# Differential-attention scores as pairs of half-array matmuls, both softmaxes side by side

## The reference, cut to what matters

```python
scale = DIFF_HEAD_DIM ** -0.5            # DIFF_HEAD_DIM = 64
for start in range(0, S, Q_BLOCK):       # Q_BLOCK = 128
    s = jnp.einsum('bqhrd,bkhrd->bhrqk', qb, kb).astype(jnp.float32) * scale   # r = 0, 1
    mask = jnp.arange(end)[None, :] <= (start + jnp.arange(Q_BLOCK))[:, None]
    p = jax.nn.softmax(jnp.where(mask, s, -jnp.inf), axis=-1)
    attn = p[:, :, 0] - lam * p[:, :, 1]
    outs.append(jnp.einsum('bhqk,bkhe->bqhe', attn.astype(vb.dtype), vb))
```

## Time and profile before

| | |
|---|---|
| median of three runs | 3796.17 us |
| lowest, highest | 3788.92, 3796.29 us |
| the profiled execution's own time | 3797.9 us |
| its span (first to last instruction) | 3795.5 us |
| mean granted TensorE clock | 0.993 |
| bytes moved by DMA | 799.34 MB |

### The profile page before, as it was taken

The page is one execution under the profiler, slowest core; times in us unless marked ns, Lnnn a source line. Parts: engine busy times, 40 slices in busy tenths (PEclk is TensorE's granted clock), DMA queues, the critical chain, the costliest instruction groups (busy, mean ns, idle before and its releaser), DMA issues.

```text
span 3795.5 us, 58631 instructions
## 1 busy us (share of the span) xinstructions
PE 3710.7 (98%) x24136; PEld 3092.0 (81%) x24136; DVE 1834.5 (48%) x3358; ACT 1378.4 (36%) x2500; POOL 482.8 (13%) x244
## 2 busy tenths in 40 slices
PE   8989999999999999998999999999999999999999
PEld 7878878978897887976888779888777888887887
DVE  5757534541645355557655665555654222232223
ACT  4322422231232354566656555545552200021001
POOL 2101220000000000233233430100000100000000
PEclk9999999999999999999999999999999999999999
DMA  8746677467665877866676666554424655464554
GB/s 313 266 161 228 228 269 268 178 222 239 217 216 183 281 248 233 283 213 203 223 232 233 199 212 214 173 160 162 140 110 169 238 188 187 176 240 172 190 195 160
DMA packets 198874, 799.34 MB, mean 211 GB/s; under 512 B 20816, under 2 KB 70224, under 8 KB 130384
## 3 DMA queue, kind: packets, MB, share of 16 engines
q1 hardware_dynamic: 198608, 795.59, 60.3%
HBM read 594.18 MB, written 201.33 MB: 210 GB/s over the span
## 4 chain that ended last, share of the span: by engine, by line
PE 90%; DVE 4%; ACT 2%; DMA 1%; issue 1%; SPq 0%; POOL 0%; DVEq 0%; ACTq 0%
PE bank L1402 86%; PE bank L1406 4%; DVE P L2484 1%; DVE P L2486 1%; DVE R L2145 0%; SPq L2688 0%; ACT P L1940 0%; ACT P L1939 0%; ACT slot L1823 0%; POOL slot L2648 0%; DMA zraw<-in_x_t_dram 0%; DMA R<-X1d 0%; DMA slot<-Wd 0%; DVE Z1a L2192 0%; ACT L1939 0%
## 5 line engine op out<-in xcount | busy, mean ns | idle before, releaser
L1402 PE MATMUL bank<-Z1a,slot 128*128 128x512 f32 x3048 | 781.6, 401 | 9.5 <-DVE slot L2083 9.5
L1402 PE MATMUL bank<-Z1b,slot 128*128 128x512 f32 x3048 | 785.2, 402 | 4.0 <-DVE Z1b L2192 3.8
L1402 PE MATMUL bank<-slot,Z0b 128*128 128x512 f32 (+1 forms) x3504 | 708.7, 353 | 8.1 <-DVE AF L2214 5.3
L1402 PEld LDWEIGHTS bank<-Z1b,slot 128*128 128x128 f32 x3048 | 567.3, 189 | 139.7 <-issue 7.5
L1402 PEld LDWEIGHTS bank<-Z1a,slot 128*128 128x128 f32 x3048 | 566.0, 189 | 140.0 <-DVE slot L2083 9.5
L1402 PEld LDWEIGHTS bank<-slot,Z0b 128*128 128x128 f32 x3504 | 562.8, 189 | 101.1 <-DVE AF L2214 6.0
L2648 POOL TENSOR_TENSOR slot<-raw,slot 128x1024 fp32r<-128x1024 f32 x117 | 308.2, 2642 | 676.7 <-ACT slot L1823 676.6
L2145 DVE SCALAR_TENSOR_TENSOR R<-bank,small,R 128x512 f32<-128x512 f32 x352 | 260.9, 749 | 208.4 <-PE bank L1402 207.8
L1402 PE MATMUL bank<-KS,DQ 128*128 128x512 f32 (+3 forms) x960 | 281.8, 389 | 9.9 <-DMA KS<-Kd 5.5
L2452 DVE TENSOR_SCALAR_CACHE_REDUCE P<-bank 128x512 f32<-128x512 f32 (+3 forms) x320 | 189.3, 608 | 201.3 <-PE bank L1402 201.0
L2660 POOL TENSOR_TENSOR Z0b<-AF,Z0b 128x512 fp32r<-128x512 f32 x88 | 127.5, 1449 | 1235.9 <-ACT Z0b L2013 1235.9
(11 more groups left out here) (235 smaller groups left out, 4560.8 us busy)
## 6 DMA issues: line engine op xcount, KB each, us to landing
slot<-Wd SPq DMA_DIRECT2D x390, 1024.0 KB, 4.9
Wd<-slot SPq DMA_DIRECT2D x130, 1024.0 KB, 7.4
raw<-in_wts_dram SPq DMA_DIRECT2D x130, 512.0 KB, 4.2
DQ<-Qd SPq DMA_DIRECT2D x192, 128.0 KB, 3.7
DV<-Vd SPq DMA_DIRECT2D x60, 256.0 KB, 4.6
KS<-Kd SPq DMA_DIRECT2D x24, 512.0 KB, 7.3
KS<-Kd SPq DMA_DIRECT2D x24, 384.0 KB, 7.0
zraw<-Yd SPq DMA_DIRECT2D x16, 512.0 KB, 5.0
```

The costliest lines, as they stand in the source:

```text
L1402: return e.matmul(o, a, b, start=start, stop=stop, skip_group_check=True)
```

## The change

For diff heads, `scores` for r = 0 only waits, and for r = 1 a new function `score_pair` computes chunk c of both softmaxes. KS is laid out the other way round: softmax 0's keys lie in partitions 0 to 63, softmax 1's in 64 to 127, the high parts in one buffer and the low parts in another. DQ holds softmax 0's query parts in partitions 0 to 63 and softmax 1's in 64 to 127, in two slots. Each matmul contracts 64 rows, softmax 0 in the upper half of the array and softmax 1 in the lower, into two banks. Three products are taken (high x high, low x high, high x low; low x low is left out), two matmuls each. In the last chunk both masks come first. VectorE waits for softmax 1's signal for both. The planner's `front` has c outside and r inside, new modelled costs, one slack of 2000 ns in place of 300, and asks for the next head's second K part after the unit's last chunk of both softmaxes. Stick-breaking heads keep their matmuls. NKS is a name for the three buffers.

```diff
@@ -41,6 +41,7 @@
 N_TILES = 64 + N_F
 NSLOT, NRAW = 4, 2
 C_CUT = 14
+NKS = 3
 
 
 class Signal:
@@ -199,7 +200,7 @@
             for qt in range(NT)]
 
 
-SLACK_H, SLACK_C, SLACK_F, SLACK_B = 1500.0, 2000.0, 300.0, 2500.0
+SLACK_H, SLACK_C, SLACK_F, SLACK_B = 1500.0, 2000.0, 2000.0, 2500.0
 
 
 class Order:
@@ -646,6 +647,7 @@
         self.banks.remove(6)
         yield ("ev", self.user[6])
         P.put(("att",), ("pool", 200), ("dve", 600))
+        held = [0.0, 0.0]
         for u, (s, e, half, qt) in enumerate(self.units):
             i = self.heads.index((s, e))
             if (half, qt) == (0, 0):
@@ -658,32 +660,31 @@
                 yield ("tr", u - 2, (NT * self.units[u - 2][0] + self.units[u - 2][3]) // 4)
             n = SUB * s + 128 * (qt + 1)
             ws = chunks(n)
-            for r in ((0, 1) if e < 4 else (half,)):
-                yield max(P.end[("ld", i, "k", r)], P.end[("ld", i, "q", qt)])
-                for c, w in enumerate(ws):
-                    m = len(self.chunk_no)
-                    self.chunk_no[u, r, c] = m
-                    if m > 1:
-                        yield t2
-                    if m:
-                        t2 = t1
+            yield max([P.end[("ld", i, "k", r)] for r in ((0, 1) if e < 4 else (half,))] + [P.end[("ld", i, "q", qt)]])
+            for c, w in enumerate(ws):
+                for r in (0, 1) if e < 4 else (half,):
+                    self.chunk_no[u, r, c] = len(self.chunk_no)
+                    if e >= 4 or r == 0:
+                        yield held[0 if e < 4 else -2]
+                    if e >= 4:
+                        pe = 30 + 0.92 * w + (60 if c == len(ws) - 1 else 0)
                     else:
-                        t2 = 0.0
-                    ev = ("dve", 90 + 1.2 * w) if e < 4 else ("act", 400 + 1.7 * w)
-                    t1 = P.put(("sc", u, r, c), ("pe", 30 + 0.92 * w + (60 if c == len(ws) - 1 else 0)), ev,
-                               after=P.clock["pe"])
-                if qt == NT - 1 and r == 0:
-                    self.get(i + 1, ("k", 1))
-                if r == 1:
-                    self.get(i + 1, ("q", qt))
-                if e < 4:
-                    t = P.put(("ex", u, r), ("dve", 120), ("act", 500 + 0.9 * n), after=t1)
+                        pe = 80 + 1.37 * w + (120 if c == len(ws) - 1 else 0) if r else 0
+                    t = P.put(("sc", u, r, c), ("pe", pe), ("dve", 90 + 1.2 * w) if e < 4 else ("act", 400 + 1.7 * w),
+                              after=P.clock["pe"])
+                    held = [held[1], t]
+            if qt == NT - 1:
+                self.get(i + 1, ("k", 1))
+            if e < 4 or half:
+                self.get(i + 1, ("q", qt))
             if e < 4:
+                for r in range(2):
+                    t = P.put(("ex", u, r), ("dve", 120), ("act", 500 + 0.9 * n), after=t)
                 yield t
                 P.put(("cb", u), ("dve", 900 + 1.1 * n), after=t)
             else:
-                yield t1
-                P.put(("cb", u), ("dve", 300 + 3.5 * n), after=t1)
+                yield t
+                P.put(("cb", u), ("dve", 300 + 3.5 * n), after=t)
 
     def back(self):
         P = self.P
...
@@ -1336,7 +1337,7 @@
 
             s, e = HEADS[i]
             u = UNITS.index((s, e, 0 if e < 4 else r, qt))
-            return pe_sc("sc", u, r, len(chunks(SUB * s + 128 * (qt + 1))) - 1)
+            return pe_sc("sc", u, r if e >= 4 else 1, len(chunks(SUB * s + 128 * (qt + 1))) - 1)
 
         def last_values(i, g):
             s, e = HEADS[i]
@@ -1591,18 +1592,42 @@
                 n = SUB * s + 128 * (qt + 1)
                 ws = chunks(n)
                 w, at = ws[c], sum(ws[:c])
-                ks = KS[plan.kloads.index((i, r)) % 3]
-                b = bank[2 + plan.chunk_no[u, r, c] % 2]
                 if u == 0:
                     first_layer_done(pe)
                 if (free := score_free(u, r, c)) is not None:
                     pe.wait_ge(*free)
-                pe.wait_ge(*d_ks[plan.kloads.index((i, r)) % 3]("ld", i, "k", r))
                 pe.wait_ge(*d_dq[qt]("ld", i, "q", qt))
+                if e_ < 4:
+                    if r == 1:
+                        score_pair(u, c)
+                    return
+                ks = KS[plan.kloads.index((i, r)) % NKS]
+                b = bank[2 + plan.chunk_no[u, r, c] % 2]
+                pe.wait_ge(*d_ks[plan.kloads.index((i, r)) % NKS]("ld", i, "k", r))
                 mm(b[:, 0:w], DQ[:, qt, 2 * r, :], ks[:, at:at + w], True, False)
                 if c == len(ws) - 1:
-                    mm(b[:, w - 128:w], ident_bf[:, :], mask_bf[:, 0 if e_ < 4 else 1, :], False, False)
+                    mm(b[:, w - 128:w], ident_bf[:, :], mask_bf[:, 1, :], False, False)
                 mm(b[:, 0:w], DQ[:, qt, 2 * r + 1, :], ks[:, at:at + w], False, True).then_inc(*pe_sc.inc("sc", u, r, c))
+
+            def score_pair(u, c):
+
+                s, e_, half, qt = UNITS[u]
+                i = HEADS.index((s, e_))
+                ws = chunks(SUB * s + 128 * (qt + 1))
+                w, at = ws[c], sum(ws[:c])
+                m = [plan.kloads.index((i, part)) % NKS for part in range(2)]
+                b = [bank[2 + plan.chunk_no[u, r, c] % 2][:, 0:w] for r in range(2)]
+                last = c == len(ws) - 1
+                if last:
+                    for r in range(2):
+                        mm(b[r][:, w - 128:w], ident_bf[:, :], mask_bf[:, 0, :], True, False)
+                for n, (q, k) in enumerate(((0, 0), (1, 0), (0, 1))):
+                    pe.wait_ge(*d_ks[m[k]]("ld", i, "k", k))
+                    for r in range(2):
+                        h = slice(64 * r, 64 * r + 64)
+                        x = mm(b[r], DQ[h, qt, q, :], KS[m[k]][h, at:at + w], n == 0 and not last, n == 2)
+                        if n == 2:
+                            x.then_inc(*pe_sc.inc("sc", u, r, c))
 
             def transposes(u, g):
                 st = ("tr", u, g)
@@ -2444,7 +2469,7 @@
                     return
                 ws = chunks(SUB * s + 128 * (qt + 1))
                 at, w = sum(ws[:c]), ws[c]
-                dve.wait_ge(*pe_sc("sc", u, r, c))
+                dve.wait_ge(*pe_sc("sc", u, 1, c))
                 if r == 0:
                     probabilities_free(dve, u)
                 elif u:
@@ -2790,17 +2815,17 @@
                 s, e_ = HEADS[i]
                 if what == "k":
                     m = plan.kloads.index((i, x))
-                    if m >= 3:
-                        sp.wait_ge(*last_score(*plan.kloads[m - 3], NT - 1))
+                    if m >= NKS:
+                        sp.wait_ge(*last_score(*plan.kloads[m - NKS], NT - 1))
                     else:
                         first_layer_done(sp)
                     for z in range(s + 1):
                         stored(z, 2 + 2 * e_ if e_ < 4 else 6 + 2 * e_, 0)
                     n = SUB * (s + 1)
-                    d = d_ks[m % 3]
-                    for part in range(2):
-                        to = KS[m % 3][64 * part:64 * part + 64, 0:n].bitcast(F32)
-                        transfer(to, Kd[e_, 64 * x:64 * x + 64, part, 0:n], d, "ld", i, what, x)
+                    for y in range(2):
+                        h, src = (x, y) if e_ >= 4 else (y, x)
+                        to = KS[m % NKS][64 * y:64 * y + 64, 0:n].bitcast(F32)
+                        transfer(to, Kd[e_, 64 * h:64 * h + 64, src, 0:n], d_ks[m % NKS], "ld", i, what, x)
                 elif what == "q":
                     if i:
                         sp.wait_ge(*last_score(i - 1, 1, x))
@@ -2808,6 +2833,10 @@
                         first_layer_done(sp)
                     stored(s, 3 + 2 * e_ if e_ < 4 else 7 + 2 * e_, 0)
                     for rep in range(2):
+                        if e_ < 4:
+                            h = slice(64 * rep, 64 * rep + 64)
+                            transfer(DQ[h, x, 0:2, :].bitcast(F32), Qd[e_, NT * s + x, h], d_dq[x], "ld", i, what, x)
+                            continue
                         to = DQ[64 * rep:64 * rep + 64, x, :, :].bitcast(F32).rearrange("p (h a) t -> p h (a t)", h=2)
                         transfer(to, Qd[e_, NT * s + x].rearrange("(h p) a t -> p h (a t)", h=2), d_dq[x],
                                  "ld", i, what, x)
```

## The result

The changed kernel took 3846.64 us (median of 4 runs, 3843.97 to 3847.32), against 3794.88 us for the kernel before beside it: a ratio of 1.0137, 95% interval 1.0121 to 1.0153. That is some 52 us slower. Forecast were 3829 us and slower by 33, with 3764 to 3856 as the range. The direction held, and so did the price of the split; the size forecast was two thirds of the one measured, and some 30 us of the loss come from a stall that the sum had at 0.

A forecast was written before the change was run, and what follows sets the result against it. PE was taken to bound the kernel; -31.9 + 62.4 - 3.7 + 6 = +32.8 us on the profiled 3797.9 us gave 3830.7, and 3829 us as that execution lies 1.7 us above the median; range 3764 to 3856.

The forecast's parts named there:

- Bound: Whole kernel: TensorE (PE), busy 98% of the span, sets the time; no other engine is busy more than half.
- Part 1: Diff-head score chunks: three side-by-side pairs of half-array matmuls replace four full ones, saving one pitch a chunk, -31.9 us.
- Part 2: Going into and out of the split at each score chunk: array emptying and exposed weight loads, 0.390 us times 160, +62.4 us.
- Rival B: Score chunks: row halves need no emptying, so the split's edges cost 0 to 16.8 us; 3767 to 3783 us, chance 0.25.
- Part 3: Masks in a unit's last chunk: both come first instead of between products, saving 0.240 - 0.182 us a unit, -3.7 us.
- Part 4a: Pairs waiting for DVE to empty both score banks: main-lane parts cover it, 0; 58 us if the cover were gone.
- Part 4b: Second K part's later load at the 12 diff-head boundaries: about 0.5 us of wait each, +6 us, bounds 0 and 36.
- Part 4c: Larger slack makes attention finish later, but 920 us of other work follow: 0, with +-10 us for the shuffled order.
- Part 4d: Q loads of diff heads halve, the DMA queue isn't the bound, DVE and ACT do the same work: 0.

The follow-up runs named there:

- a_two: Changed kernel without its second pair (query low part times key high part), so two pairs a chunk: 3819.62 us, ratio 1.007.
- a_mask_mid: Changed kernel with the two masks between the first and second pair, one more way out of and into the split per unit: 3866.0 us, ratio 1.0189.
- a_early: Changed kernel with front-lane slack of 300 ns until sub-sequence 0's units are placed, then 2000 ns: 3816.77 us, ratio 1.0062; 3815.6 when run again.
- full_early: Changed kernel with the old full-array matmuls and K and Q layout, slack 300 ns for sub-sequence 0, then 2000 ns: 3800.51 us, ratio 1.0022.
- a_full: Changed kernel with four full-array products per chunk from the old K and Q layout; order, 2000 ns slack and joint banks stay: 3836.41 us, ratio 1.0109.
- b_early: Kernel before, full matmuls, with slack of 300 ns for sub-sequence 0, then 2000 ns: 3792.44 us, ratio 0.9994.
- a_seq: Changed kernel with a chunk's three half matmuls of softmax 0 first, then three of softmax 1: 3846.51 us, ratio 1.0144.

## Why the prediction was right in direction and short in size

**Bound (held).** PE set the time; both parts of the loss are PE's, one busy and one idle.

**Part 1, -31.9 us (held).** Pairs run side by side; a pair is worth 29.6 us of PE's busy time in a_two.

**Part 2, +62.4 us (held step by step).** The timeline gives 0.095, 0.10, 0.09 and 0.10 at one chunk, and a_mask_mid gives 0.30 us in total time for one more excursion, through two masks. The column split was the right row to price the row split by. Rival B, at 0.25, needed 0.23 and 0.46 where the trace has 0.32 and, from the last pair to the second full matmul, about 0.66.

**Part 3, -3.7 us (sign right, undersized).** The emptying after a 128-column mask took 0.150, not the 0.202 that I had taken from 128-column transposes: a mask pair costs 0.05 us less a unit, 64 x 0.05 = 3 us. Parts 1 to 3 so come to 23.5, against 21.8 of busy time and 15 between the medians in the clean order.

**Part 4a, 0 (held for this slack).** PE's own waits for VectorE's evictions went from 1.5 to 4.3 us, 2.3 of it in the stall; with 300 ns they were 8.9. I did not look at the banks that ScalarE empties, where PE's waits went from 2.8 to 7.7 us; in a_early they are 2.3.

**Part 4b, +6 us (too large).** I read 9.4 us as PE's wait for K loads. That sum counts the loader's wait too; PE's own was 5.5 us, and it became 6.7, 1.2 more. It was not spread over twelve boundaries either: of its two waits one was 5.14 us, in the stall, and in a_early one wait of 2.1 us is left.

**Part 4c, 0 (the step that failed).** I wrote that the larger slack makes attention finish later and that "it has room at the end". I looked at the last sub-sequence only, and for that one it was nearly right: a_early ends its scores 275 us later than the kernel before and has no more idle time. The first one to be needed is sub-sequence 0, and its projection follows the second layer's other projections directly. It had 48 us of room, and its operand became ready 61 us later while the main lane came earlier. The slack alone costs 16 us in the old kernel. In the changed one a_early, which keeps the slack short for sub-sequence 0 alone, takes 30 us back. My bound of +-10 us, read off the idle time of before, bounded what a better order can give, not what a worse one can take. That was the error of reasoning: idle time now is no bound for idle time after.

**Part 4d, 0 (not so in the stall).** I wrote that the DMA queue isn't the bound, from its mean share. At the stall it was: the store and the load of the heads stood 9.3 us and 1.8 us in SP's queue after what they needed was there (1555.7 to 1564.96, and 1572.85, when the store had landed, to 1574.67), and the load took 15.2 us. No run parts the late heads from the full queue; moving the heads forward removed both.

**Clock.** I had no term for it. PE stood idle for 3.92 us before 1565.94; the granted clock fell to half, the lower of its two levels (1.2 and 2.4 GHz), at 1567.4 us and was there in three stretches between 1500 and 1610. They are these windows of the changed kernel:

```profile
1567.40:1570.80 3.40, 3.40 (x16) 3.31 (x16) 0.00 (x0) 0.32 (x1) 0.69 (x1) 0.50 0.91 289
1574.20:1594.70 20.50, 11.24 (x51) 7.62 (x52) 6.06 (x26) 7.89 (x16) 2.36 (x1) 0.50 0.75 249
1601.50:1604.90 3.40, 3.40 (x19) 3.40 (x18) 0.69 (x1) 0.00 (x0) 0.00 (x0) 0.50 0.02 5
```

The timeline shows the price: fourteen value products took 1.83 us from 1560.19, sixteen took 3.68 us from 1567.28, 0.12 and 0.22 us from start to start. So half of the 18.0 us in which PE was busy in these windows, 9 us, is lost on top of the idle time (an estimate). The half clock lies inside the stall and not behind it. It fits the 12.0 us of busy time that a_early takes back; full_early and a_early, whose windows from 1500 to 1610 us have a clock of 1.00, show the split's 21.8 us of busy time without it.

**Sum as measured.** Split 15 to 22 us, stall with its clock 30 us, joint order 8 us: 53 to 60, for 52. In the late order the split adds 10 us between medians and 14.3 in busy time; the intervals of the ratios do not part 10 from 15.

**What was luck.** The direction was not luck: with the stall taken out, a_early is still 22 us slower than the kernel before. That 3829 lies within 18 us of the result is luck in part: parts 1 to 3 and 4b were 10 to 17 us too large, 4c was 30 us too small, and the joint order's 8 us stood nowhere.

**What stays open.** Why the joint order costs 8 us without the split. At the start of attention, from 1246 to 1500 us, PE is idle for 15.9 us in full_early (the row below) and for 9.1 in the kernel before (254 less 244.87, above), 6.8 more; but from 1610 to 1800 us it is idle 11.2 us less (5.5 for 16.8), and over the whole span 3.8 us more, so this does not explain it. No run tells either why the long slack costs 33 us with the joint order (1.0109 for a_full, 1.0022 for full_early) and 16 without.

```profile
1246.00:1500.00 254.00, 238.07 (x1576) 206.68 (x1575) 114.24 (x293) 106.27 (x270) 5.46 (x3) 0.97 0.77 252
```

A fourth K buffer, which would undo part 4b, was not tried.

No version found here beats the kernel before. b_early is level with it, and all versions with a split are slower.

## What to carry to other kernels

Half-array tiling is cheap inside a split and dear at its edges: here 0.39 us an excursion, against one pitch of at most 0.232 us saved by it. By these two numbers it would pay from two 512-column chunks per excursion on (0.46 us saved), an estimate that no run tests; it takes more PSUM banks than the two that this kernel has for scores. When a stage is made later by a scheduler's constant, look for its first consumer, not its last, find how long its operand lies ready before it is used, and look at the DMA queue there and not at its mean. And before an idle time is taken from a view, see whether it adds up two engines.

## What was not expected of the hardware

Matmuls of the two row halves run side by side in both program orders tried, three deep: with three of the upper half queued ahead of three of the lower one, each lower one started 10 to 17 ns after its upper counterpart, 2 to 4 ns when they alternate. The Trainium skill, TensorE: Matmul & The Clock Gate, The mechanism, says that matmuls keep program order in start and end with no reordering; in a_seq the fourth matmul of the program must have started before the second for two to start together at 2449.88, so the measurement decides against it for different row groups. The Trainium skill, on the same page under Measured speedup vs the span model, prices a pack of tiles at one matmul and some 4 ns for each further tile, which this trace shows as 2 to 4 ns.
